# The inversion of the heads' triangular blocks, with matmuls over 32x32 blocks in place of 64x64

## The reference

```
def step(state, inp):
    r_t, w_t, k_t, v_t, a_t, b_t = inp
    sa = einsum('bhvk,bhk->bhv', state, a_t)
    state = state * w_t + sa[..., None] * b_t + v_t[..., None] * k_t
    y = einsum('bhvk,bhk->bhv', state, r_t)
```

## Time and profile before

| what | value |
|---|---|
| time, median of 3 runs | 3258.43 us (3256.69 to 3261.16) |
| span of the profiled execution | 3254.1 us |
| mean granted TensorE clock in it | 0.974 |
| TensorE busy | 3029.2 us, 93% of the span |
| VectorE, ScalarE, GpSimd busy | 1840.2, 1393.4, 669.5 us |
| the 8 merge stretches | 207.07 us |
| the 8 dense stretches behind them | 143.18 us |

### The profile page before, as it was taken

One profiled execution on the slowest core, in us unless ns is written; L12 is line 12 of the kernel. 1 busy time (PEld: TensorE's weight loads), 2 busy tenths in 40 slices (PEclk: granted clock), 3 DMA queues, 4 the chain that ended last, 5 costly groups with the idle time before them and its releaser, 6 DMA issues. The chain is left out here.

```text
span 3254.1 us, 59877 instructions
## 1 busy us (share of the span) xinstructions
PE 3029.2 (93%) x25454; PEld 2407.3 (74%) x25454; DVE 1840.2 (57%) x2665; ACT 1393.4 (43%) x2369; POOL 669.5 (21%) x542
## 2 busy tenths in 40 slices
PE   8989999999978999999989999989788989699999
PEld 6757788887746788887658888767577777588887
DVE  6665533445665543445665736474376867457464
ACT  5555322235455422234464424345465655344242
POOL 1000311211000311212001101133275746011010
PEclk9989999999999999999999999989899999899999
DMA  4101333222101322322012323235411111133232
GB/s 148 52 2 67 103 97 97 92 96 84 52 5 64 99 95 94 97 94 77 1 53 92 109 84 101 88 107 192 142 48 30 49 36 42 48 97 108 80 98 83
DMA packets 82344, 260.72 MB, mean 80 GB/s; under 512 B 9632, under 2 KB 13216, under 8 KB 81824
## 3 DMA queue, kind: packets, MB, share of 16 engines
q1 hardware_dynamic: 71424, 235.39, 22.6%
q10 hardware_dynamic: 10656, 21.50, 1.7%
HBM read 235.89 MB, written 20.97 MB: 79 GB/s over the span
## 5 line engine op out<-in xcount | busy, mean ns | idle before, releaser
L1696 DVE TENSOR_TENSOR mlp_w_lo<-mlp_ring,mlp_w_hi 128x1024 fp32r<-128x1024 f32 (+1 forms) x211 | 251.7, 1193 | 576.8 <-ACT mlp_w_hi L1673 576.7
L1673 ACT ACTIVATE mlp_w_hi<-mlp_ring 128x1024 fp32r<-128x1024 f32 (+1 forms) x211 | 213.2, 1011 | 646.1 <-PE ps L1634 639.2
L1696 DVE TENSOR_TENSOR ffn_w_lo<-ffn_ring,ffn_w_hi 128x1024 fp32r<-128x1024 f32 (+3 forms) x172 | 224.1, 1303 | 443.0 <-ACT ffn_w_hi L1673 443.0
L1673 ACT ACTIVATE ffn_w_hi<-ffn_ring 128x1024 fp32r<-128x1024 f32 (+3 forms) x172 | 187.2, 1089 | 485.9 <-PE ps L1634 480.2
L1633 PE MATMUL ps<-mlp_more_parts,mlp_w_hi 128*128 128x512 f32 x952 | 373.1, 392 | 0.0
L1632 PE MATMUL ps<-tiles_parts,mlp_w_hi 128*128 128x512 f32 x832 | 329.7, 396 | 1.1 <-issue 1.1
L1632 PE MATMUL ps<-ffn_x_parts,ffn_w_hi 128*128 128x512 f32 x792 | 312.4, 395 | 17.8 <-DVE ffn_x_parts L2411 14.2
L1634 PE MATMUL ps<-tiles_parts,mlp_w_lo 128*128 128x512 f32 x832 | 327.7, 394 | 0.0
L1632 PE MATMUL ps<-mlp_more_parts,mlp_w_hi 128*128 128x512 f32 x760 | 305.4, 402 | 21.0 <-DVE mlp_w_lo L1696 12.6
L1633 PE MATMUL ps<-ffn_x_parts,ffn_w_hi 128*128 128x512 f32 x792 | 309.9, 391 | 0.0
L1634 PE MATMUL ps<-ffn_x_parts,ffn_w_lo 128*128 128x512 f32 x792 | 309.9, 391 | 0.0
(11 more groups left out here) (504 smaller groups left out, 6166.2 us busy)
## 6 DMA issues: line engine op xcount, KB each, us to landing
ffn_ring<-in_w_ffn_up SPq DMA_DIRECT2D x88, 512.0 KB, 3.5
mlp_ring<-in_w_up SPq DMA_DIRECT2D x64, 512.0 KB, 3.6
mlp_ring<-in_w_down SPq DMA_DIRECT2D x64, 512.0 KB, 3.5
rwkv_keep<-ffn_ring ACTq DMA_DIRECT2D x64, 256.0 KB, 2.4
sq<-rwkv_keep SPq DMA_DIRECT2D x64, 256.0 KB, 3.1
ffn_ring<-in_w_ffn_down SPq DMA_DIRECT2D x16, 768.0 KB, 4.3
in_ring<-in_w_in SPq DMA_DIRECT2D x22, 512.0 KB, 3.6
mlp_ring<-in_w_in SPq DMA_DIRECT2D x22, 512.0 KB, 3.5
```

The costliest lines, as they stand in the source:

```text
L1673: nc.scalar.activation(w.w_hi[:, n % SPLIT, 0:width], w.ring[:, n % RING, 0:width], ACT.Copy).then_inc(s["w_hi_ready"], 1)
L1696: nc.vector.tensor_tensor(w.w_lo[:, n % SPLIT, 0:width], w.ring[:, n % RING, 0:width], w.w_hi[:, n % SPLIT, 0:width].bitcast(F32), ALU.sub ...
```

## The change

`inner` and `outer` multiply 32x32 blocks and leave out those that are zero. At levels 0 to 3 only the four diagonal 32x32 blocks of a 128-partition tile hold anything, so there are 4 matmuls for each instance in place of 2. At level 4 only one off-diagonal block of each chunk is filled, so there are 2 for each instance, as before, but of 32x32. The PSUM banks, the copies, the transposes, the masks and all semaphores stay as they are; the copies still move 256 columns.

```
+BW = HD // 2
...
+        def blocks(level):
+            for i in range(4):
+                if level < RW_LEVELS - 1:
+                    for b in range(4):
+                        rows, at = slice(b * BW, (b + 1) * BW), slice(b % 2 * BW, (b % 2 + 1) * BW)
+                        yield i, rows, at, rows, at
+                else:
+                    for b in (0, 2):
+                        yield i, slice(b * BW, (b + 1) * BW), slice(0, BW), slice((b + 1) * BW, (b + 2) * BW), slice(BW, HD)
...
                 def inner(c, t, level):
...
-                    for i in range(4):
-                        for chunk in (half(0), half(1)):
-                            mm = nc.tensor.matmul(m.ps[chunk, t % 2, packed(i)], NM[chunk, u % PARTS_AHEAD, i, :], XT[chunk, t, i, :],
-                                                  start=True, stop=True, skip_group_check=True)
+                    for i, into, at, rows, over in blocks(level):
+                        mm = nc.tensor.matmul(m.ps[into, t % 2, i * HD + over.start:i * HD + over.stop], NM[rows, u % PARTS_AHEAD, i, at], XT[rows, t, i, over],
+                                              start=True, stop=True, skip_group_check=True)
...
                 def outer(c, t, level):
...
-                    for i in range(4):
-                        for chunk in (half(0), half(1)):
-                            mm = nc.tensor.matmul(m.ps[chunk, 2 + t, packed(i)], X[chunk, t, i, :], T1[chunk, t % 2, i, :],
-                                                  start=False, stop=True, skip_group_check=True)
+                    for i, into, at, _, over in blocks(level):
+                        mm = nc.tensor.matmul(m.ps[into, 2 + t, i * HD + over.start:i * HD + over.stop], X[into, t, i, at], T1[into, t % 2, i, over],
+                                              start=False, stop=True, skip_group_check=True)
```

## The result

The changed kernel took 3360.42 us (median of 4 runs, 3346.36 to 3364.42), the kernel before in the same session 3257.56 us (4 runs, 3253.94 to 3261.16). The ratio is 1.0303, with an interval of 1.0287 to 1.0320: some 103 us slower. The forecast was 3323 us in a range of 3285 to 3385, so the sign was right, the time lies in the range, and the loss was over half as large again as forecast: 103 us in place of 65. The time lies above the forecast's own bounds (3293 to 3345 us) and inside the range only by the room that the range kept for the rival of the lasting low clock.

What follows compares the result with a forecast made beforehand. Instruction delivery, about 3.7 us a block of 251, was taken to bound the dense stretches, with merge stretches at its edge. Span 3254.1 + 57 (added blocks) + 8 (clock) = 3319 us, plus 4.3 outside it: 3323 us, range 3285 to 3385.

Steps and rivals of the forecast that it cites:

- rival of the lasting low clock: Starved merge stretches keep the array at 1.2 GHz through dense and thin stretches, 8 us an iteration: around 3379 us, chance 0.12.
- The mechanism: In merge and dense stretches, PE's instructions arrive in blocks of 251 loads and matmuls, about 3.7 us each; added instructions cost time.
- Delivery is not the limit: Rival: the dense stretches' stalls have another cause and PE simply loses 8.1 us an iteration; around 3228 us, chance 0.12.
- a floor of 15 ns a pair: Rival: no delivery limit, levels 0 to 3 cost the same, level 4 gives 1.8 us an iteration; about 3253 us, chance 0.04.
- reading of the dense stretches: Dense stretches are bound by instruction delivery: 3.77 us a block, where the array at 15 ns a pair would need 1.9.
- price of 3.7 us: Delivery time charged per block of 251 loads and matmuls in merge and dense stretches; bounds 3.5 and 3.9 us.
- sum over the blocks: Merge and dense stretches together: 115.9 blocks, eight at 1 us, the rest at 3.7, 407.2 us against 350.25: +57 us.
- the block that was to be free in each iteration: One block already there when each merge stretch begins, since the thin stretch before uses few instructions; charged 1 us.
- slack: Merge stretches take 4.5 us a block where 3.7 would do, so part of the added blocks' 121 us is hidden.
- clock term: Stalls in merge stretches lower the clock, paid at the dense stretch's end and the wide matmuls behind it: 8 us.
- Array time: In `inner` and `outer`, 32x32 pairs over four tiles take 8.3 ns each; the change saves 8.1 us an iteration.
- Changing the tile size: Some 14 changes an iteration between 64x64 and 32x32, 0 to 0.1 us each, at most 11 us; taken as 0.

Runs made afterwards that it cites:

- filler run: Changed kernel plus ten 128x128-by-512-column matmuls on constants an iteration, which nobody reads: 3363.76 us, ratio 1.0329 against the kernel before.
- half-instances run: Changed kernel with only instances 0 and 1 of four multiplied, in 32x32 blocks, at levels 0 to 3: 3262.46 us, ratio 1.0022 against the kernel before.
- run with half of the added instructions: Changed kernel with levels 0 and 1 put back to 64x64 blocks, 32x32 at levels 2 to 4: 3313.07 us, ratio 1.0170 against the kernel before.
- half of the 64x64 instances: Kernel before, 64x64 blocks, with instances 2 and 3 left out at levels 0 to 3: 3249.44 us, ratio 0.9982.
- extra pairs: Kernel before plus one 32x32 matmul on constants ahead of each 64x64 one of levels 0 to 3: 4420.51 us, ratio 1.3572.
- split-columns run: Changed kernel, but levels 0 to 3 keep 64x64 weights, each matmul issued as two streaming 32 columns: 3405.05 us, ratio 1.0455 against the kernel before.

## Why the prediction was right in sign and short in size

**The mechanism held.** A block of instructions is delivered at a pace of its own, and PE stands when it asks faster. The pauses, all at the borders of blocks, the packets 3.6 us apart, the filler run (+48 us of PE work, 0 us of time in the merge stretches) and the half-instances run (same form, no added instructions, merge stretches of 206 us) show it from four sides. It was there before: the 20 pauses of over 0.5 us without a semaphore in the trace of before lie at block borders too. "Delivery is not the limit" and "a floor of 15 ns a pair" are out: neither has a place for 94 us that vanish with the instructions. Most signs that the prediction named came: 235 packets (236 forecast), x4608 at `inner`, "issue" as the main entry, dense stretches of 19 to 20 us. Two came otherwise: the steady merge stretches take 36 to 39 us (the last, of the final iteration, 39.85), not 33, and the pauses last 1.7 us on average, with 18 of 71 at 2 us or more.

**The reading of the dense stretches was too strong.** The prediction took all of their 3.77 us a block as the pace of delivery, since the array would need 1.9 us. The 1.9 us take each pair at 15 ns, and not all are so short:

```profile
2615.28 1.80 PE L2712 MATMUL ps<-heads_R,heads_state 64*64 64x64 f32 x56
```

That is (1.80 - 0.22) / 55 = 29 ns, and `u0` has the same spacing; a transpose has 0.11 us. With some 120 pairs at 29 ns, 490 at 15 and 24 at 110 I estimate 13.5 us for the 5.1 blocks of a steady dense stretch, some 2.6 us a block. PE paused at 11 of the 37 borders there, for 12.5 of 143.18 us in all. The price of 3.7 us still came out near, for the packets' spacing of 3.7 us says the same; that 3.77 agreed with it is in part luck.

**The step that failed is the sum over the blocks.** At 3.7 us a block, 32.6 more blocks are 121 us. The forecast let 64 of these disappear: 350.25 us before against (83.3 - 8) x 3.7 + 8 = 287 us that its formula gives for the blocks of before. Of these 64 us, 22 were the block that was to be free in each iteration, and 40 the distance between the merge stretches' 4.5 us a block and 3.7, read as slack that more instructions would fill. Measured, the merge stretches grew by 93.8 us, so 27 us disappeared.

- A block does lie ready, but it saves little. At the first border in the merge stretch PE pauses for no more than 0.34 us in seven of the eight stretches, and for 1.69 in the eighth. But this border comes 0 to 3.2 us behind the stretch's start, and from it to the next one it takes 3.45 to 5.63 us, 4.06 on average, as long as everywhere, and at the second border PE pauses in all eight. So one block lay ready, and no second one.
- The slack is no reserve. The run with half of the added instructions shows a straight line from the first block on, 2.8 to 2.9 us each. A likely reason, which no run isolates: PE's waits for DVE, ACT and POOL lie partly beside the delivery and partly ahead of it, and a block that is entered late is also asked for late. Why a block then comes out at 3.86 us by the count (300.85 us for 77.9 blocks of 251) and 3.99 by the intervals, and not at the packets' best spacing of 3.6, was not taken apart further.

In the terms of the prediction: 450.0 us for 115.9 blocks, 3.88 us each over all of them, in place of 3.7 with eight at 1 us. The price makes 0.18 x 115.9 = 21 us of the 43 that were missing over merge and dense stretches, the eight blocks at 1 us the other 22. Of the 43, 5 to 6 us are the clock's and stood in a term of their own, so 37 were short, which is what the medians miss (3360 against 3323).

**The clock term was right in size.** 8 us were forecast, and the dense stretches give 6.0. The pauses at their block borders don't make these: they fell from 12.5 to 6.5 us. The time at 1.2 GHz, worked out from the granted clock, does fit. In the kernels whose dense stretches are unchanged, 3 to 9 us of it in the eight of them go with 140.8 to 143.2 us (before, half of the 64x64 instances, extra pairs), 27 us with 144.2 (full fillers), and 30 to 43 us with 149.1 to 150.9 (all others). This comparison isn't an experiment on the clock alone. The thin stretches, which had a part in the forecast's 8 us, lost nothing. The rival of the lasting low clock was half true: the clock was low for most of each merge stretch, (1 - 0.57) / 0.5 of it or 32 of 37 us, but was back within the dense one (0.81 to 0.91 over it), so that the time that the rival asked for didn't come. Where the array isn't the bound, the clock cost little: the merge stretches take 301 us both at 0.55 to 0.59 and, with fillers, at 0.86 to 0.95.

**Array time was a little off, without effect.** A 32x32 pair in four tiles was taken as 8.3 ns. At the full clock, 64 of them took 0.79 us in the filler run, (0.79 - 0.18) / 63 = 9.7 ns; at the low clock, (1.07 - 0.24) / 63 = 13 ns. **Changing the tile size** was taken as 0 to 0.1 us. In the timeline above, the run at 2591.03 starts 0.36 us after the last 64x64 group, whose like start 0.21 us apart: 0.15 us. For some 15 changes an iteration that is at most 18 us if nothing hid it; most does lie under the delivery, since the half-instances run has these changes too and its merge stretches are no longer than those of before. Its exact share was not isolated.

**A rule against a row.** The page "Runtime: NRT & Kernel Launch" of the Trainium skill, "Instruction fetch mechanics", holds the crossing of a block to be mostly hidden. The measurement decides against it here: PE stood at "issue" for 96.5 us in this part. Its block of 256 instructions is borne out: all 72 pauses of over 0.6 us without a semaphore lie at one position modulo 256.

## What to carry to other kernels

Count instructions as a resource with a price of its own: in this kernel a stretch in which TensorE gets through 251 of its loads and matmuls in under 3.7 to 3.9 us waits for their delivery, and every further one cost some 12 ns (94 us for 8192), however small its tile. Smaller blocks pay only if they keep the number of instructions; wider ones pay only if a wide one doesn't hold the array for more than the narrow ones that it replaces. To find this limit, divide PE's instructions by the packets of the instruction queue, and look for pauses on "issue" inside a run of one operation and for the packets' spacing beside them. Count at how many borders of blocks TensorE really pauses before you call a stretch bound by delivery: 11 of 37 in the dense stretches of before, 71 of 78 in the merge stretches of after. And don't take the distance to the limit for slack unless a run has filled it.

## What was unexpected of the hardware

- Tiles of different sizes hardly overlapped: alternating 64x64 and 32x32 matmuls cost 0.28 us a change at a granted clock of 0.51, six times the 47 ns that a pair of one size took at 0.56 (57.33 us for 1233 in the split-columns run).
- With 64 columns of weights, streaming 32 columns in place of 64 saved nothing (29 ns a pair over two tiles, so 59 a tile, either way); with 32x32 weights the same 32 columns held a tile for 4 x 9.7 = 39 ns. The 32x32 matmuls also have half the rows, so whether rows or width of the weights made the difference isn't shown.
- Matmuls of 64 rows by 128 weight columns with 128 streamed columns started 59 ns apart, although they alternate between the two halves of the rows.
- In a stretch that the array doesn't bound, the granted clock hardly mattered: 301 us both at 0.55 to 0.59 and at 0.86 to 0.95. In one that it does bound, of the split-columns run, 37 us at 0.99 became 58 at 0.56.
- TensorE resumed 2.15 to 2.90 us behind the start of the packet that it waited for, at all 71 pauses of the merge stretches after, and the next packet started 1.1 to 2.8 us after it had resumed.
